# Moving the weight buffers and the activation buffers by 32 bytes in SBUF, in a two-block transformer kernel on one core

## The chip, the cores and the metric

The kernel runs on one core of a Trainium2 chip. The time is the device time of one launch in microseconds (us), lower is better. Three runs of the kernel before gave 3391.88, 3397.97 and 3398.14 us, median 3397.97 us.

## What is computed

Two blocks of depth 2 follow each other on an activation `x` of 256 tokens by 1024 channels, all in 32-bit floating point. Cut to what matters, with `modulated` a scaled and shifted RMS norm:

```python
# block 1, i = 0 and 1
x = x + 0.5 * gate * (silu(h @ w_gate) * (h @ w_up)) @ w_down      # h = modulated x, 1024 -> 2816 -> 1024
x = x + gate * (ssd_mixer(h) if i == 0 else mla_mixer(h))           # w_in, w_out
x = x + 0.5 * gate * (silu(h @ w_gate) * (h @ w_up)) @ w_down
# block 2, l = 0 and 1
x = x + gate * concat(rwkv7(h @ w_in), pool(h @ w_in)) @ w_out
x = x + gate * peer_ffn(h)     # queries, top 16 of 128 x 128 experts for each of 8 heads
# peer_ffn: act = gelu(h . peer_u[e]);  out = sum_e gate_e * act_e * peer_v[e]
```

The expert layer is computed densely here: all 16,384 rows of `peer_u` and of `peer_v` pass through TensorE, and the gates of experts that weren't chosen are zero.

## The kernel before

**Layout.** Activations stand with channels on the 128 partitions and the 256 tokens along the free axis, so one channel tile is 128x256, 1,024 bytes in each partition. Weights come from HBM as blocks of 128x1024 (512 KB, 4,096 bytes in each partition), one after the other over SyncE's queue, into slots: four slots of `ring`, and in some stages up to eight more (`MORE`) that lie inside `arena`, a buffer of 128 KB per partition that also holds every stage's temporary tensors. A block is eight 128x128 weight tiles of 512 bytes per partition.

**Weights in two parts.** Most products are made in the format fp32r, with one pass of TensorE instead of fp32's several, and in three parts so that the precision holds. ScalarE copies a block rounded to `weights_hi` (four buffers, line 1143). VectorE subtracts it from the block and leaves the rest, the low part, in place of the block (line 1638; `ring`, or `more_lo` for the slots in the arena). An activation is split the same way: `hh` (h_hi) and `h` (h_lo) for the normalized input of a stage, `small` (gat_hi) and `work` (gat_lo) for the gated activations that go into the second half of an FFN or of the expert layer.

**The matmuls around the change.** `columns_in_parts` (line 514) is the product of a weight block with the stage's input. For each of eight channel tiles it makes three matmuls of 128x256 moving columns: (high weights, `hh`), (high weights, `h`), (low weights, `hh`). `front` (lines 526, 527, 540) does the same for the first three blocks of a stage in another order. `rows_in_parts` (line 547) is the second half of an FFN and of the expert layer: three matmuls for each tile, with `small`, `work`, `small` as moving operands. In the output projections of two mixers (lines 681, 692 and 811) the moving operand lies in `more_lo`. Each of these matmuls loads its own 128x128 stationary tile (LDWEIGHTS, shown as PEld), and the load for the next one runs beside the current one.

**Order.** TensorE, ScalarE and VectorE each run a list in program order, bound by semaphores: a block's landing, its high part, its low part, its use (`block_used`, after which its slot may be filled again). In the four FFN stages VectorE also multiplies 56 blocks of modulation weights, which come over GpSimd's queue (line 1566). In the expert layers VectorE also does the routing (lines 2008 to 2075) and builds the gate matrix beside the first half (lines 2098 to 2113).

**Addresses.** `build` takes the buffers one after the other with `sb(...)`. Each begins at the next address that is a multiple of 32 bytes, so a buffer `[P, 2]` of 8 bytes moves what follows by 32 bytes. `sb_twice` lays a second view over the same bytes. In this kernel `ring` begins at byte 16,512 of a partition, which is a multiple of 128. The tiles that the matmuls named above read lie at multiples of 128 bytes from their buffer's start, so for them a whole buffer has one position modulo 128.

Of the kernel before, what the change touches and what calls it, by code (L numbers as in the profile page):

```python
# [8 lines left out]
F32R = mybir.dt.float32r  # L9
# [7 lines left out]
P = 128  # L17
D = 1024
T = 256
DT = D // P  # L20
# [246 lines left out]
def build(nc, stream, mods, cols_d, consts_d, x_d, pos_d, wuq_d, wukv_d, cond_d, keys_d, pool_d, lora_d, gup_d, vup_d, acts_d, out_d):  # L267
    with ExitStack() as ctx:
        def sb(name, shape, dt=F32):
            return ctx.enter_context(nc.sbuf_tensor(name, shape, dt))  # L270
# [6 lines left out]
        def sb_twice(name, shape, parts):  # L277

            with nc.sbuf_tensor(name, shape, F32) as whole:
                pass  # L280
            return whole, [sb(f"{name}_{i}", p, dt) for i, (p, dt) in enumerate(parts)]

        ring, (ring_lo,) = sb_twice("ring", [P, RING, 1024], [([P, RING, 1024], F32R)])
        whi = sb("weights_hi", [P, WS, 1024], F32R)
        with nc.sbuf_tensor("arena", [P, 128, 256], F32) as AR:
# [1 line left out]
        sb("arena_low", [P, 30, 256])  # L287
        more_lo = sb("more_lo", [P, MORE, 1024], F32R)
        sb("arena_high", [P, 128 - 30 - 4 * MORE, 256])
        x = sb("x", [P, DT, T])  # L290
        vfirst = sb("vfirst", [P, 4, T])
        cols = sb("cols", [P, NCOLS])
        kept = sb("kept", [P, KEPT])
# [2 lines left out]
        eps = sb("eps", [P, 20])  # L296
        modc = sb("modc", [P, NSUB, 24])
        omk = sb("one_minus_k_a", [P, 8])
        sb("ahead_of_activations", [P, 2])
        h, (h_lo,) = sb_twice("h", [P, DT, T], [([P, DT, T], F32R)])  # L300
        hh, (h_hi,) = sb_twice("hh", [P, DT, T], [([P, DT, T], F32R)])
        work, (_, gat_lo) = sb_twice("work", [P, 2048], [([P, 1024], F32), ([P, 4, T], F32R)])

        small, (gat_hi, _) = sb_twice("small", [P, 5, T], [([P, 4, T], F32R), ([P, T], F32)])

        ijg, rs, rv = small[:, 0:3, :], small[:, 3, :], small[:, 4, :]
        PS = ctx.enter_context(nc.psum_tensor("psum", [P, 8, 512], F32))
        acc = PS[:, 4:8, :].rearrange("p b (s t) -> p (b s) t", s=2)
# [2102 lines left out]
```

## Time and profile before

| | |
|---|---|
| median of three runs | 3397.97 us (3391.88 to 3398.14) |
| the profiled execution | 3391.88 us, span 3390.0 us |
| TensorE matmul busy | 3251.1 us, 96% |
| TensorE weight load busy | 3108.9 us, 92% |
| VectorE busy | 2581.1 us, 76% |
| ScalarE busy | 1608.2 us, 47% |
| mean granted TensorE clock | 0.987 of full speed |
| HBM traffic | 208 GB/s over the span |

The span runs from the first to the last instruction; 1.88 us of the profiled execution lie around it. The profiled execution is the fastest of the three runs, 6.1 us under their median. Rows of matmuls overlap in the profile: a row of 276 ns is followed by the next start 113 ns later, so what a stream of matmuls costs is read from the distance of starts, or from how many start in a stretch, not from the length of a row.

### The profile page before, as it was taken

The numbers are of one execution on the slowest core, as the hardware profiler recorded it, in microseconds if no ns is written. First come the engines' busy times: TensorE is split into PE (matmuls) and PEld (weight loads), VectorE is DVE, ScalarE is ACT, GpSimd is POOL, SyncE is SP. The second block draws the span as 40 slices with busy tenths as digits, with TensorE's granted clock in tenths as the row PEclk, the third lists the DMA queues.
The fourth block names the chain that finished last, engine by engine and source line by source line (L and its number), as shares of the span: only waits on it lengthen the run. The fifth ranks groups of instructions, "written<-read, shape, count | busy, mean of one in ns | idle before, by whom it ended". The sixth has DMA issues, their size and how long they took to land.

```text
span 3390.0 us, 68787 instructions
## 1 busy us (share of the span) xinstructions
PE 3251.1 (96%) x26804; PEld 3108.9 (92%) x26804; DVE 2581.1 (76%) x4576; ACT 1608.2 (47%) x2594; POOL 196.5 (6%) x331
## 2 busy tenths in 40 slices
PE   6999989999999998999999999998899999999998
PEld 5999769999867997989999999998789999999998
DVE  7989667989836997747978777776846978877777
ACT  3466644454445445144455444445325445544444
POOL 1100001111100111200000000000300000000000
PEclk8999999999999999999999999999999999999999
DMA  9964218979603973045755477774114665567775
GB/s 373 385 225 166 73 50 337 391 283 387 269 20 124 397 299 130 7 162 189 235 199 177 169 240 237 231 233 159 63 67 167 234 221 183 172 211 234 232 234 184
DMA packets 246578, 707.46 MB, mean 209 GB/s; under 512 B 27472, under 2 KB 93008, under 8 KB 244928
## 3 DMA queue, kind: packets, MB, share of 16 engines
q1 hardware_dynamic: 212112, 571.64, 48.4%
q0 software_dynamic: 34224, 132.46, 10.1%
q8 instruction: 167, 2.74, 0.3%
q14 instruction: 75, 0.61, 0.1%
HBM read 669.40 MB, written 34.60 MB: 208 GB/s over the span
## 4 chain that ended last, share of the span: by engine, by line
PE 81%; DMA 7%; DVE 6%; ACT 3%; issue 2%; SPq 0%; POOL 0%; DVEq 0%; ACTq 0%
PE psum L514 34%; PE psum L547 27%; DMA ring<-stream 6%; PE psum L1071 3%; PE psum L893 2%; PE psum L1006 1%; PE psum L644 1%; DVE ring L1638 1%; PE psum L913 1%; PE psum L495 1%; ACT weights_hi L1143 1%; PE psum L526 1%; PE psum L527 1%; DVE arena L1696 1%; PE psum L728 1%
## 5 line engine op out<-in xcount | busy, mean ns | idle before, releaser
L514 PE MATMUL psum<-hh,weights_hi 128*128 128x256 f32 x4216 | 1189.2, 282 | 24.5 <-DVE ring L1638 12.0
L1143 ACT ACTIVATE weights_hi<-ring 128x1024 fp32r<-128x1024 f32 x711 | 752.7, 1059 | 955.7 <-DMA ring<-stream 895.6
L1638 DVE TENSOR_TENSOR ring<-ring,weights_hi 128x1024 fp32r<-128x1024 f32 x711 | 870.2, 1226 | 409.5 <-ACT weights_hi L1143 404.6
L514 PE MATMUL psum<-h,weights_hi 128*128 128x256 f32 x4216 | 1172.2, 278 | 0.0
L514 PE MATMUL psum<-hh,ring 128*128 128x256 f32 x2976 | 829.0, 279 | 0.0
L514 PEld LDWEIGHTS psum<-hh,weights_hi 128*128 128x128 f32 x4216 | 796.6, 189 | 34.3 <-DVE ring L1638 17.2
L514 PEld LDWEIGHTS psum<-h,weights_hi 128*128 128x128 f32 x4216 | 798.7, 189 | 0.3
L547 PE MATMUL psum<-small,weights_hi 128*128 128x256 f32 x2752 | 768.8, 279 | 2.6 <-DVE ring L1638 1.6
L547 PE MATMUL psum<-work,weights_hi 128*128 128x256 f32 x2752 | 765.9, 278 | 0.0
L547 PE MATMUL psum<-small,ring 128*128 128x256 f32 x2304 | 642.2, 279 | 0.0
L514 PEld LDWEIGHTS psum<-hh,ring 128*128 128x128 f32 x2976 | 563.3, 189 | 0.0
L547 PEld LDWEIGHTS psum<-small,weights_hi 128*128 128x128 f32 x2752 | 520.5, 189 | 5.9 <-DVE work L2113 2.9
L547 PEld LDWEIGHTS psum<-work,weights_hi 128*128 128x128 f32 x2752 | 517.9, 188 | 0.0
L547 PEld LDWEIGHTS psum<-small,ring 128*128 128x128 f32 x2304 | 432.5, 188 | 0.0
L514 PE MATMUL psum<-hh,more_lo 128*128 128x256 f32 x1240 | 342.9, 277 | 0.0
L1638 DVE TENSOR_TENSOR more_lo<-arena,weights_hi 128x1024 fp32r<-128x1024 f32 x214 | 261.1, 1222 | 49.6 <-ACT weights_hi L1143 46.4
L1566 DVE SCALAR_TENSOR_TENSOR arena<-arena 128x1024 f32<-128x1024 f32 x232 | 282.3, 1219 | 5.1 <-DMA arena<-mod_weights 3.9
L1143 ACT ACTIVATE weights_hi<-arena 128x1024 fp32r<-128x1024 f32 x214 | 225.3, 1055 | 100.4 <-PE psum L514 75.3
L514 PEld LDWEIGHTS psum<-hh,more_lo 128*128 128x128 f32 x1240 | 232.8, 188 | 0.0
L2098 DVE TENSOR_SCALAR work<-kept,small 128x128 f32<-128x128 f32 x512 | 142.6, 343 | 71.2 <-PE psum L1071 65.9
L2109 DVE TENSOR_TENSOR work<-work,arena 128x256 f32<-128x256 f32 x256 | 159.6, 625 | 0.0
L2180 POOL DMA_DIRECT2D arena<-mod_weights x208 | 109.8, 528 | 529.9 <-DVE arena L1566 526.4
(410 smaller groups left out, 3894.0 us busy)
## 6 DMA issues: line engine op xcount, KB each, us to landing
ring<-stream SPq DMA_DIRECT2D x735, 512.0 KB, 3.9
arena<-mod_weights POOLq DMA_DIRECT2D x224, 512.0 KB, 7.0
arena<-stream SPq DMA_DIRECT2D x222, 512.0 KB, 6.4
acts<-small SPq DMA_DIRECT2D x256, 128.0 KB, 2.2
work<-acts SPq DMA_DIRECT2D x256, 128.0 KB, 3.0
arena<-cond_rows POOLq DMA_DIRECT2D x3, 1024.0 KB, 7.1
arena<-w_uq POOLq DMA_DIRECT2D x1, 3072.0 KB, 10.6
arena<-constants POOLq DMA_DIRECT2D x2, 1200.0 KB, 5.7
```

The source lines that it names most:

```text
L495: mm = pe.matmul(PS[:, 2, 0:T], ones, SQ[:, d, :], start=(d == 0), stop=(d == DT - 1))
L514: mm = pe.matmul(out, lhs[:, d, :], rhs[:, d, :], start=(d == 0 and p == 0), stop=(d == DT - 1 and p == 2))
L526: pe.matmul(out, w[:, d, :], h_hi[:, d, :], start=opens and d == 0, stop=False, skip_group_check=True)
L547: mm = pe.matmul(acc[:, d, :], lhs[:, d, :], rhs, start=False, stop=False, skip_group_check=True)
L893: mm = pe.matmul(PS[:, (4 * st + b) % 8, j * P:(j + 1) * P], lhs[:, c, :], rhs[:, c, :], start=True, stop=True)
L1071: mm = pe.matmul(PS[:, 4 + g % 4, j * P:(j + 1) * P], OHI[:, g % 2, j, :], OHJ[:, g % 2, j, :], start=True, stop=True)
L1143: act.activation(whi[:, NTH[n] % WS, :], raw(n), ACT.Copy).then_inc(sem["block_hi"], 1)
L1566: return dve.scalar_tensor_tensor(PRODUCT[:, m % 2, :], block, 1.0, COND[:, 0 if g < 6 else 1, :], ALU.mult, ALU.mult, accum_out=modc[:, g ...
L1638: dve.tensor_tensor(low(n), raw(n), whi[:, NTH[n] % WS, :].bitcast(F32), ALU.subtract)\
L2098: dve.tensor_scalar(OHI[:, g % 2, j, :], iota, ijg[:, 0, t:t + 1], ijg[:, 2, t:t + 1], ALU.is_equal, ALU.mult)
L2109: dve.tensor_tensor(gat[:, k % 4, :], sil[:, k % 4, :], WALL[:, :, i * 4 + k], ALU.mult).then_inc(sem["pe_gated"], 1)
L2180: pool.dma_start(MODRING[slot], mods[i * MOD_RING + (first + slot + MOD_RING)]).then_inc(mod_full[slot], 16)
```

## The change

Nothing is computed differently, no instruction is added or taken out, and no order, semaphore or DMA changes. Only the addresses of buffers in SBUF change.

```diff
+        sb("line_half", [P, 2])
         ring, (ring_lo,) = sb_twice("ring", [P, RING, 1024], [([P, RING, 1024], F32R)])
         whi = sb("weights_hi", [P, WS, 1024], F32R)
@@
         sb("arena_high", [P, 128 - 30 - 4 * MORE, 256])
+        sb("line_rest", [P, 2])
         x = sb("x", [P, DT, T])
+
+        h, (h_lo,) = sb_twice("h", [P, DT, T], [([P, DT, T], F32R)])
+        hh, (h_hi,) = sb_twice("hh", [P, DT, T], [([P, DT, T], F32R)])
         vfirst = sb("vfirst", [P, 4, T])
@@
         omk = sb("one_minus_k_a", [P, 8])
-        sb("ahead_of_activations", [P, 2])
-        h, (h_lo,) = sb_twice("h", [P, DT, T], [([P, DT, T], F32R)])
-        hh, (h_hi,) = sb_twice("hh", [P, DT, T], [([P, DT, T], F32R)])
+
         work, (_, gat_lo) = sb_twice("work", [P, 2048], [([P, 1024], F32), ([P, 4, T], F32R)])
```

The start of each buffer modulo 128 bytes, counted from the sizes above and the steps of 32:

| buffer | before | after |
|---|---|---|
| `ring`, `weights_hi`, `arena`, `more_lo` | 0 | 32 |
| `x` | 0 | 64 |
| `h`, `hh` | 64 | 64 |
| `vfirst`, `cols` | 0 | 64 |
| `kept` (identity, ones) and `zeros` | 96 | 32 |
| `work`, `small`, `ident_bf16` | 64 | 96 |

The moving operand's position less the stationary operand's, modulo 128, called the distance from here on:

| matmuls | before | after |
|---|---|---|
| lines 514, 526, 527, 540 (moving `hh` or `h`) | 64 | 32 |
| line 547 (moving `small` or `work`) | 64 | 64 |
| lines 681, 692, 811 (moving `more_lo`) | 0 | 0 |

## Rows read from the trace of the kernel before

**Rows 1.** The page: busy time of each engine (us, share, instructions).
```profile
PE 3251.1 (96%) x26804; PEld 3108.9 (92%) x26804; DVE 2581.1 (76%) x4576; ACT 1608.2 (47%) x2594; POOL 196.5 (6%) x331
```

**Rows 2.** The chain that ended last, in order of time: start us, us, what, whole span.
```profile
52.47 111.52 PE psum L514 x984
163.99 57.13 PE psum L547 x504
...
735.75 111.52 PE psum L514 x984
...
1567.34 4.25 DMA ring<-stream
...
1673.89 3.80 DMA ring<-stream
...
1687.00 37.03 PE psum L514 x312
...
2552.74 36.76 PE psum L514 x312
...
2597.37 121.56 PE psum L514 x1032
...
3019.82 266.38 PE psum L547 x2280
```

**Rows 3.** Groups by line, whole span: xcount | busy us, mean ns of one | idle before.
```profile
L514 PE MATMUL psum<-hh,weights_hi 128*128 128x256 f32 x4216 | 1189.2, 282 | 24.5 <-DVE ring L1638 12.0 <-ACT arena L1357 8.8 <-DVE more_lo L1638 1.9
...
L514 PE MATMUL psum<-h,weights_hi 128*128 128x256 f32 x4216 | 1172.2, 278 | 0.0
...
L514 PE MATMUL psum<-hh,ring 128*128 128x256 f32 x2976 | 829.0, 279 | 0.0
...
L514 PE MATMUL psum<-hh,more_lo 128*128 128x256 f32 x1240 | 342.9, 277 | 0.0
```

**Rows 4.** Timeline of TensorE at 120 us: start us, us, what.
```profile
119.74 0.28 PE L514 MATMUL psum<-h,weights_hi 128*128 128x256 f32 x1
...
120.99 0.28 PE L514 MATMUL psum<-hh,weights_hi 128*128 128x256 f32 x1
```

**Rows 5.** Timeline of TensorE at 510 us, distance 0.
```profile
509.79 0.28 PE L692 MATMUL psum<-more_lo,weights_hi 128*128 128x256 f32 x1
...
510.99 0.28 PE L692 MATMUL psum<-more_lo,ring 128*128 128x256 f32 x1
```

**Rows 6.** Groups by line from 60 to 160 us, matmuls.
```profile
L514 PE MATMUL psum<-hh,weights_hi 128*128 128x256 f32 x295 | 81.4, 276 | 0.0
```

**Rows 7.** Groups by line from 2570 to 2720 us, matmuls.
```profile
L514 PE MATMUL psum<-hh,weights_hi 128*128 128x256 f32 x403 | 113.3, 281 | 0.0
```

**Rows 8.** Groups by line from 490 to 528 us, matmuls.
```profile
L692 PE MATMUL psum<-more_lo,weights_hi 128*128 128x256 f32 x192 | 35.3, 286 | 4.7 <-DVE ring L1638 4.7
```

**Rows 9.** Stretches: us, busy and count of PE, PEld, DVE, ACT, POOL, then clock, DMA share, GB/s.
```profile
60.00:160.00 100.00, 100.00 (x885) 100.00 (x884) 94.52 (x137) 44.57 (x58) 19.34 (x37) 1.00 1.00 386
...
2600.00:2700.00 100.00, 100.00 (x851) 100.00 (x850) 89.34 (x377) 45.79 (x70) 0.00 (x0) 1.00 0.69 231
1960.00:2060.00 100.00, 100.00 (x851) 99.98 (x850) 74.17 (x106) 47.85 (x71) 0.00 (x0) 1.00 0.71 235
```

**Rows 10.** Timeline of TensorE at 1022 us, four transposes merged in one row.
```profile
1022.50 0.60 PE L783 MATMUL psum<-kept,arena 128*128 128x128 f32 x4
```

**Rows 11.** Groups by line from 1021 to 1027 us, the same transposes.
```profile
L783 PE MATMUL psum<-kept,arena 128*128 128x128 f32 x8 | 1.2, 272 | 0.0
```

**Rows 12.** Groups by line, whole span: two VectorE operations of one shape.
```profile
L2067 DVE TENSOR_TENSOR arena<-arena,kept 128x2048 f32<-128x2048 f32 x8 | 18.3, 2284 | 0.0
L2071 DVE TENSOR_TENSOR arena<-arena 128x2048 f32<-128x2048 f32 x8 | 18.3, 2284 | 0.0
```

**Rows 13.** The stretch of the second FFN's first half, line 514: us, PE, clock, DMA share, GB/s.
```profile
547.00:658.30 111.30, 110.71 (x976) 1.00 1.02 400
```

## The prediction

> **What bounds the kernel now.** I read the page first. TensorE is busy for 96% of the span and its weight loads for 92%, VectorE for 76% [rows 1]. Busy time can't tell a fast stream of matmuls from a slow one, since the rows overlap. So I went to the chain that ended last, in order of time, and divided each long piece by its count [rows 2]. The reader is to see long stretches in which nothing but TensorE's own pace sets the time: 984 matmuls in 111.52 us (113.3 ns each), twice, and 504 in 57.13 us (113.4 ns). But the same instruction is slower elsewhere: 312 in 36.76 us and 1032 in 121.56 us (117.8 ns both), 312 in 37.03 us (118.7 ns), and of line 547 2280 in 266.38 us (116.8 ns). The counts of whole stretches say the same: 885 matmuls in 100 us (113.0 ns) against 851 in 100 us (117.5 ns), all three at granted clock 1.00, the full 2.4 GHz, with TensorE busy throughout [rows 9]. So there are two paces of one instruction, about 113.3 and 117.8 ns, and neither clock nor waiting makes the difference.
>
> A third pace shows where the moving operand lies in `more_lo`: ten intervals in 510.99 - 509.79 = 1.20 us, 120 ns [rows 5], against eleven in 120.99 - 119.74 = 1.25 us, 113.6 ns by the rounded starts [rows 4]. The length of a row goes with the pace: 276 ns in the fast stretch, 281 in the slow one, 286 at line 692 [rows 6 to 8]. The last has distance 0, the first two distance 64. I read it as two streams out of SBUF, the moving tile and the next stationary tile, that get in each other's way, more or less according to where they lie. That the distance does it is my reading; line 692 differs from line 514 in its tensor too.
>
> The least pace that a 256-column matmul could have is bounded by rows in which nothing of this shows. Four fp32 transposes of 128 columns take 0.60 us [rows 10], each row 272 ns long [rows 11], so (600 - 272) / 3 = 109 ns apart. Scaling by columns is no help here, as fp32 takes more passes; but their row of 272 ns is 4 ns under the fast 276 and their pace 4 ns under 113.3, so I take 113.3 - 4 = 109.3 ns as the floor.
>
> The Trainium skill has a sentence on exactly this (TensorE: Matmul & The Clock Gate, Part 2, the step on LDWEIGHTS): "Loading the next tile's weights doesn't steal SBUF read bandwidth from the running matmul." Its gap for a warm 256-column matmul, N / 2.4 + 2.5, is 109.2 ns. The trace doesn't agree with the second: no stretch of line 514 runs under 113.0 ns [rows 9]. By the first, no placement of the two operands could matter, and the change would be worth nothing; that is the second rival below.
>
> **The change part by part.**
> (1) Lines 514, 526, 527, 540. Line 514 has 4216 + 4216 + 2976 + 1240 = 12,648 matmuls [rows 3]; `front` adds 24 x 3 x 10 = 720. Together 13,368. Their distance goes from 64 to 32. What pace have they now? The slow pieces in the chain hold 312 + 312 + 1032 = 1,656 [rows 2], smaller ones are cut off; I take 2,000, so the mean is 113.3 + 4.5 x 2,000 / 13,368 = 114.0 ns. Distance 32 stands nowhere in the trace for this instruction. Bounds: the floor 109.3 (gain 13,368 x 4.7 = 63 us) and the pace at distance 0, 120 (loss 13,368 x 6.0 = 80 us). The transposes are the nearest rows with half-way positions (`kept` at 96 against `arena` at 0), and show no collision; but their loads may differ, so they aren't proof. Between the ends far apart I choose by a supposition, not by a row: if the streams are read in pieces of 64 bytes, distances 0 and 64 both put the starts of the pieces on each other, and 32 is the first that puts them in between. I take the middle of the fast pace and the floor, 111.3 ns: 13,368 x 2.7 = 36 us gained.
>
> (2) Line 547, 3 x 8 x (4 x 22 + 2 x 128) = 8,256 matmuls. The distance stays 64; both operands move by 32. I price it at nothing. It can come out in either pace whatever the placement: 504 at 113.4 and 2280 at 116.8 exist side by side [rows 2]. If all ran fast, the second kind, some 3,700, would give back 17 us; if all ran slow, 4,500 more would cost 20 us.
>
> (3) Lines 681, 692, 811: distance 0 before and after, 576 matmuls, nothing.
>
> (4) VectorE, ScalarE, GpSimd. Every operand in the arena, `ring` and `weights_hi` moves from 0 to 32. An operation that reads `kept` (position 96) beside the arena takes 2284 ns, one of the same shape with the arena alone 2284 ns too [rows 12]. So nothing; and VectorE, with 74 to 94.5% busy [rows 9], would hide the first percent. Where it doesn't hide is the FFNs: at 94.5% their length can shrink by 5.5% at most, and the 1.8% of (1) fits, the 3.5% of the floor just does.
>
> (5) DMA. Weight blocks now land at 32 instead of 0. In the first half of an FFN the DMA engines are full (share 1.02, 400 GB/s) while TensorE is still busy for 110.71 of 111.30 us [rows 13]. No row shows a block landing at another position. Below, nothing; above, if each percent of slower landing came out in full in four such stretches, 4 x 111 x 1% = 4.5 us for a percent. I take nothing.
>
> (6) What isn't passed on. In the first expert layer's first half the chain goes through `DMA ring<-stream` again and again, in 13 pieces of about 4 us from 1567.34 to 1673.89 us [rows 2]. There a faster TensorE waits longer for its block. I take a tenth off: 36 becomes 32 us.
>
> Sum: the profiled execution 3391.9 - 32 = 3360 us. It lies 6 us under the median of its three runs, so against medians 3366; I put the forecast between, 3364 us, 1.0% faster than 3397.97.
>
> **The rivals.**
> *A, the collision falls at distance 32 (the forecast).* For it: the pace depends on placement at all, 113.3 against 120 [rows 4, 5], and nothing says that 64 is the best place. Against: only whole multiples of 64 have been seen. 3325 to 3385 us.
>
> *B, the placement isn't what sets the pace.* Then the three paces come from how the streams lock onto each other after a stall, and 120 at line 692 has another cause. For it: two paces at one and the same distance, [rows 6, 7]. The rule of the Trainium skill above leads here as well. Then the time moves only as the stretches fall into one pace or the other: all fast, -(2,000 x 4.5 + 17,000) ns = -26 us; all slow, 11,368 x 4.5 ns + 20 us = +71 us. The latter would need the FFNs too, which have kept the fast pace through 984 in a row twice. 3372 to 3420 us, the middle at 3398.
>
> *C, distance 32 collides like distance 0, on the other side.* The place is line 514, the price up to 6.0 ns for each of 13,368. At 120 ns 3398 + 80 = 3478 us; at 116.7, half-way between the paces at 64 and 0, 2.7 x 13,368 = 36 us, 3434 us. It decides from the point at which the mean pace of line 514 is over 114.5 ns (0.5 x 13,368 = 7 us, 0.2%). For it: if pace grows steadily from 113.3 at 64 to 120 at 0, then 32 lies between. Against: the two distances differ by half a period, and of two streams of unequal speed each crosses the other anyway, so a steady growth isn't given.
>
> **How the numbers follow.** A 0.41, B 0.29, C 0.30. A's time is the prediction. The range should leave out two in ten: below 3325 lies only the floor with line 547 all fast (0.03), above 3440 the worse half of C (0.14). So 3325 to 3440 us; A's own range is 3325 to 3385 us. 0.2% is about what a measurement can tell from no change here. Faster: A whole and 0.11 of B, 0.52; within 0.2%: 0.10 of B, 0.10; slower: C and 0.08 of B, 0.38.
>
> **What would show it.** From 60 to 160 us, with the same instructions, the count is now 885. At 111.3 ns it is 898, at 109.3 it is 915, at 120 it is 833. The mean row length of line 514 there goes from 276 towards 272 if A is right, towards 286 if C is. Under B it stays at 276 or jumps to 281. Line 692's starts stay 120 ns apart by (3), and line 547 keeps its paces of 113 and 118; if it has a third pace, the position and not the distance matters, and step (2) is wrong. Step (4) is wrong if line 1638 or 1143 changes its mean length. Step (5) shows in idle time of TensorE before line 514, released by the DMA, between 547 and 658 us. The prediction fails most easily in (1), whose price stands on no row of its own.

## The result, and the profile after

The changed kernel takes 3415.5 us (3415.0 to 3422.48 in three runs) against 3397.97 us before: ratio 1.0066, 95% interval 1.0049 to 1.0083. It is slower by 0.66%, where 1.0% faster was forecast. The profiled execution took 3425.5 us, with a span of 3423.6 us; it is a fourth one, 10 us above the median of the three, while the profiled execution before was 6 us under its median. In `kernel.py` the lines of these matmuls stand two further down than before: line 514 is now 516, line 547 is 549.

The chain of the changed kernel, in order of time (start us, us, what):

```profile
52.40 114.80 PE psum L516 x984
167.20 57.15 PE psum L549 x504
...
507.92 20.61 PE psum L694 x168
...
745.10 114.80 PE psum L516 x984
...
2042.97 238.87 PE psum L549 x2040
...
2580.35 36.41 PE psum L516 x312
...
2624.63 78.42 PE psum L516 x672
```

The two stretches of 984 matmuls, 113.3 ns each before [rows 2], now take 114.80 us, 116.7 ns each. The stretch of 504 in the FFN's second half, where the distance was kept, is unchanged at 113.4 ns. The 312 that were slow already (117.8 ns) are at 116.7 ns too. So in these stretches both old paces of the input products are gone and a new one is in their place. The stretches of time say the same (us, busy and count of PE, PEld, DVE, ACT, POOL, clock, DMA share, GB/s):

```profile
60.00:160.00 100.00, 100.00 (x859) 100.00 (x859) 91.79 (x132) 43.20 (x54) 18.75 (x36) 1.00 0.99 377
...
547.00:658.30 111.30, 110.99 (x950) 110.74 (x950) 100.84 (x146) 51.10 (x64) 19.41 (x37) 1.00 1.01 393
```

885 matmuls in 100 us have become 859 with TensorE busy throughout and the clock granted in full [rows 9], and 976 have become 950 in the second stretch [rows 13]. VectorE and the DMA do less per microsecond because they are asked for less. The groups by line, whole span, say what else moved:

```profile
L516 PE MATMUL psum<-hh,weights_hi 128*128 128x256 f32 x4216 | 1199.4, 284 | 25.0 <-DVE ring L1640 13.6 <-ACT arena L1359 9.0 <-DVE more_lo L1640 0.9
...
L1640 DVE TENSOR_TENSOR ring<-ring,weights_hi 128x1024 fp32r<-128x1024 f32 x711 | 871.7, 1228 | 422.4 <-ACT weights_hi L1145 418.5
...
L1145 ACT ACTIVATE weights_hi<-ring 128x1024 fp32r<-128x1024 f32 x711 | 753.7, 1061 | 970.4 <-DMA ring<-stream 913.3 <-PE psum L516 39.4 <-PE psum L549 17.3
```

The mean row of these matmuls is 2 ns longer than in [rows 3], the idle time in front of them is the same (25.0 against 24.5 us). VectorE's subtraction is 1228 ns against 1226 before, ScalarE's copy 1061 against 1059.

A steady stream is measured best by the distance of successive starts. I took all distances between two neighbouring matmuls of one line from the trace, for lines 514 and 540 ("input") and for line 547. Lines 526 and 527 take turns, so they have no such neighbours and are left out. A distance of up to 125 ns counts as steady, a longer one holds a wait. "All" is the sum over both kinds.

| | input, steady | mean ns | all, us | line 547, steady | mean ns | all, us |
|---|---|---|---|---|---|---|
| before | 12,432 | 114.26 | 1506.3 | 8,198 | 115.38 | 958.9 |
| after | 12,426 | 117.07 | 1542.0 | 8,177 | 114.70 | 957.1 |

12,426 x 2.81 ns = 34.9 us more for the input products, and 8,177 x 0.68 ns = 5.6 us less for line 547, together 29.3 us. "All" grew by 35.7 us, line 547 gave back 1.8 us, together 33.9 us; the span grew by 33.6 us. So between these two executions the loss lies in the pace of the input products. The medians differ by 17.5 us only; how much of a pace reaches the time is taken up further down.

### The profile page after: what moved, and what is told of

It is laid out like the page before. It is cut to its first block, busy times and chain, and to the rows that moved or that the text cites. A ratio compares the mean times of both kernels' runs of the same rounds, so it can differ in the third digit from the quotient of the medians.

```text
span 3423.6 us, 68787 instructions
## 1 busy us (share of the span) xinstructions
PE 3283.2 (96%) x26804; PEld 3139.6 (92%) x26804; DVE 2585.0 (76%) x4576; ACT 1610.8 (47%) x2594; POOL 197.3 (6%) x331
## 3 DMA queue, kind: packets, MB, share of 16 engines
q0 software_dynamic: 34224, 132.46, 10.2%
## 4 chain that ended last, share of the span: by engine, by line
PE 80%; DMA 8%; DVE 6%; ACT 3%; issue 2%; SPq 0%; DVEq 0%; POOL 0%; ACTq 0%; POOLq 0%
PE psum L516 35%; PE psum L549 25%; DMA ring<-stream 6%; PE psum L1073 3%; PE psum L895 2%; PE psum L1008 1%; PE psum L646 1%; DVE ring L1640 1%; ACT weights_hi L1145 1%; PE psum L915 1%; PE psum L497 1%; PE psum L528 1%; PE psum L529 1%; DVE arena L1698 1%; PE psum L730 1%
## 5 line engine op out<-in xcount | busy, mean ns | idle before, releaser
L1145 ACT ACTIVATE weights_hi<-ring 128x1024 fp32r<-128x1024 f32 x711 | 753.7, 1061 | 970.4 <-DMA ring<-stream 913.3
L1640 DVE TENSOR_TENSOR ring<-ring,weights_hi 128x1024 fp32r<-128x1024 f32 x711 | 871.7, 1228 | 422.4 <-ACT weights_hi L1145 418.5
```

The source lines that it names most:

```text
L1145: act.activation(whi[:, NTH[n] % WS, :], raw(n), ACT.Copy).then_inc(sem["block_hi"], 1)
L1640: dve.tensor_tensor(low(n), raw(n), whi[:, NTH[n] % WS, :].bitcast(F32), ALU.subtract)\
```

## The experiments

Two questions had to be told apart. Is it the distance that sets the pace, or the position, or the order of the buffers? And what is the rule by which distance becomes pace?

**A map of the paces.** The network is left out; the kernel only streams matmuls of the kernel's shape and format (256 columns, fp32r, each with its own stationary tile) from buffers at chosen bytes, and its output is just the input `x`.

```diff
-            # the network
+            def run_12(bank):  # stationary at byte 0, moving at byte 48
+                for r in range(3):
+                    for w, m in tiles(0, 12, 256):     # (high, act_hi), (high, act_lo), (low, act_hi)
+                        mm = pe.matmul(PS[:, bank, 0:256], w, m, start=True, stop=True)
```

> The disputed cost by itself. This kernel leaves the whole network out (its output is the input x); it streams fp32r matmuls of 128x256 in the order of line 514 (high weights with hi, high weights with lo, low weights with hi, eight tiles, three times over), 72 after a drained start and then three times 72 with one shorter matmul of 64, 144 or 200 columns ahead of each, for 32 distances in steps of 4 bytes with the stationary tiles at byte 0 of 128, and for a few with the stationary tiles at 16, 32, 64. If the distance modulo 128 sets the pace: 113.3 or 117.8 ns at 64, about 116.7 at 32, 120 at 0, and the same numbers again when the stationary tiles begin at 32 or 64 and the moving ones are moved along. If the position of the stationary tiles inside a 64-byte piece sets it (the rival): 116.7 at every distance with the stationary tiles at 32, at 113.3 or 117.8 for every distance with them at 0. If neither does: one pair of paces, 113.3 and 117.8, everywhere. No theory says what distances 96, 80 or 48 give; if the pace is even around 64 then 96 is like 32, 116.7.

There are four stretches of 72 matmuls for each placement. The first distances of a stretch are uneven, so here and in the other maps I give the mean of a stretch without its first twelve: 120 ns at distance 0; 116.7 to 117.8 at 32; 117.8 at 64; 120 at 96; 113.3 to 113.6 at 112; 113.3 or 118.6 at 16. Distances that are no multiple of 16 gave 116.9 to 123.4 ns. With the stationary tile at byte 32 these distances gave the same paces, in another mixture at 16. With it at byte 64, distance 64 gave 113.3 ns in the first of four stretches and 117.8 in the others. So 32 is a bad distance for every position tried. But 64 was bad too, 117.8 ns in all but that one stretch, where the kernel before ran at 113.3 and I had called its distance 64. One more point solved that: at 192 the map gives 113.3 ns in three of four stretches and 117.8 in the fourth. 64 and 192 are one distance modulo 128 and two modulo 256.

**Position alone.** All buffers move by 32 bytes, weights and activations, so that no distance changes.

```diff
+        sb("all_by_32", [P, 2])
         ring, (ring_lo,) = sb_twice("ring", [P, RING, 1024], [([P, RING, 1024], F32R)])
```

> The kernel before with one 32-byte step ahead of ring, and nothing else: every buffer moves by 32, the weights begin half-way in a 64-byte piece (byte 32 of 128), the activations at 96, both distances stay 64. If the distance sets the pace, line 514 keeps 113.3 ns in the FFNs (984 in 111.5 us) and the time is that of before, 3398 within 8 us. If the stationary tiles' own position costs, line 514 and line 547 both go to 116.7 and the time is 3398 + 13,368 x 2.8 + 8,256 x 1.3 ns, about 3446 us.

3400.81 us against 3403.24 us of the kernel before on the same chip, ratio 0.9999 (0.9983 to 1.0015); mean paces 114.53 and 115.41 ns. The time doesn't move by more than the interval. But the expected 984 matmuls in 111.5 us did not come in the first FFN:

```profile
52.60 115.89 PE psum L515 x984
```

That is 117.8 ns, while the 984 of the third FFN took 111.52 us. One placement can run at either of the two paces, and nothing here shows what decides it inside the kernel.

**The changed kernel with `h` and `hh` at distance 64 again.** If the period were 128, this would undo the harm and keep the order of the buffers.

```diff
+        sb("ahead_of_h", [P, 2])
         h, (h_lo,) = sb_twice("h", [P, DT, T], [([P, DT, T], F32R)])
@@
+        sb("ahead_of_work", [P, 24])
         work, (_, gat_lo) = sb_twice("work", [P, 2048], [([P, 1024], F32), ([P, 4, T], F32R)])
```

> The changed kernel with h and hh moved on by 32 bytes, so that their distance to the weights is 64 again, and with 96 bytes ahead of work so that line 547 keeps its distance of 64. The order of the buffers stays that of the change. If the distance of line 514 is the whole cause: back to 3398 within 8 us, 984 matmuls in 111.5 us. If the new order of the buffers (h and hh ahead of vfirst, other high address bits) has a share, the time stays between 3400 and 3417.

3433.67 us, ratio 1.0085 (1.0062 to 1.0108): nothing was undone. Its chain:

```profile
52.82 115.89 PE psum L518 x984
168.72 59.37 PE psum L551 x504
```

117.8 ns in both lines, in line 547 as well, which the change had left alone and which keeps its distance modulo 128 here. My reading of distances modulo 128 fell here.

**The kernel before with only `h` and `hh` moved by 32 bytes,** its order of buffers kept.

```diff
-        sb("ahead_of_activations", [P, 2])
         h, (h_lo,) = sb_twice("h", [P, DT, T], [([P, DT, T], F32R)])
         hh, (h_hi,) = sb_twice("hh", [P, DT, T], [([P, DT, T], F32R)])
+        sb("ahead_of_gated", [P, 2])
```

> The kernel before with the 32-byte step that stood ahead of h put behind hh instead: h and hh begin at byte 32, weights at 0, distance 32, and work and small stay exactly where they were. One part of the change alone. If the distance is the cause: slower like the change, 3413 to 3425 us, 984 matmuls of line 514 in 114.8 us. If the stationary tiles' half-way position is the cause: 3398, 111.5 us.

3431.64 us, ratio 1.0082 (1.0065 to 1.0099), 117.86 ns for the input products, 115.64 ns for line 547, which kept its place. One edit of 32 bytes for two buffers costs at least as much as the whole change. It isn't the same pace, though: the two stretches of 984 took 115.46 and 116.77 us where 114.8 was expected, and the time lies above the expected 3413 to 3425 us. Modulo 256 the distance is 160, not 32.

**The period.** The same map over 512 bytes, network left out as before.

> The same measurement (the network is left out, the output is x) over distances 0 to 496 bytes in steps of 16, with all four buffers at the same byte modulo 512, 48 matmuls in each of eight stretches that begin after matmuls of different lengths; then again with both operands moved by 32. In the first map distance 64 ran at 117.8 ns in 8 stretches of 8 and distance 192 at 113.3 in 3 of 4, and distance 0 at 120.0 against 118.7 at 128. If the period is 256 bytes: 64 and 320 alike (117.8), 192 and 448 alike (113.3), 32 and 288 alike (116.7), 160 like 416, about 117.9 from the kernel with h at 32. If the period is 128, as the prediction had it, and the two paces are a matter of the start alone, 64 and 192 show the same mixture of 113.3 and 117.8. If 512: 64 differs from 320.

It repeats every 256 bytes, stretch by stretch. The means of the eight stretches (48 matmuls each, without the first twelve distances) at some distances, in ns:

| distance | eight stretches |
|---|---|
| 0, 256 and 512 | 120.0 |
| 32 and 288 | 116.7 or 116.8 in four, 117.7 or 117.8 in four |
| 64 and 320 | 117.8 |
| 112 and 368 | 113.3 in six, 113.7 in two |
| 160 and 416 | 117.3 in five, 118.7, 118.7, 120.0 |
| 192 and 448 | 113.3 in five, 117.8 in three |

At distance 192 it is always the same three stretches that run at 117.8 ns, in this map and in the two other maps of this kind, on three chips: those that follow a matmul of 144, 32 or 176 columns. After one of 64, 200, 100 or 220 columns, and after a drained start, the pace is 113.3 ns. So the choice between the two paces isn't chance there; it repeats with what went before. The lengths came in the same order in every map, so the length itself isn't shown as the cause.

Counted modulo 256 from the buffers' addresses, the kernel before has distance 192 in both lines, the changed one 32 in the input products and still 192 in line 547, and the two kernels above 64, 64 and 160, 192. The table puts the distance of the kernel before ahead of the three others, as the times do.

**Two tests of the period in the kernel,** each with 128 bytes more ahead of the activations: the changed kernel's order with distance 192, and the kernel before with distance 64.

```diff
@@ changed kernel, h and hh back on distance 64, and 128 bytes more
-        sb("ahead_of_h", [P, 2])
+        sb("ahead_of_h", [P, 34])
@@ kernel before
-        sb("ahead_of_activations", [P, 2])
+        sb("ahead_of_activations", [P, 34])
```

> The kernel of run after_h_at_96 with 128 bytes more ahead of h, so that h, hh, work and small all move by 128 and nothing changes modulo 128. If the period is 128: 3433 within 8 us, line 514 at 117.8 ns in the FFNs. If it is 256: the distance is now 192 (that of the kernel before) for both, 984 matmuls of the FFN's first half in 111.5 us, 504 of its second half in 57.1, and the time is back at 3402 within 8 us, with the order of buffers of the change.

> The kernel before with the buffer ahead of h made 128 bytes larger and nothing else: h, hh, work and small move by 128 together. If the period is 128: the time of before. If it is 256: both distances go from 192 to 64, every stretch locks into 117.8 ns, 984 in 115.9 us and 504 in 59.4, about 3434 us.

The first: 3394.71 us, ratio 0.9985 (0.9968 to 1.0002), paces 113.99 and 114.45 ns. The second: 3427.89 us, ratio 1.0087 (1.0057 to 1.0117), paces 117.10 and 117.43 ns. Chain of the first, then of the second, with the first and the third FFN:

```profile
52.28 111.52 PE psum L518 x984
163.79 57.13 PE psum L551 x504
```

```profile
52.77 115.89 PE psum L514 x984
168.66 59.37 PE psum L547 x504
...
751.34 111.52 PE psum L514 x984
```

128 bytes make the harmed kernel whole and harm the good one. The new order of buffers shows no cost. Not every stretch came to 117.8 ns in the second, as was expected: the 984 of the third FFN ran at 113.3. So 64 and 192 have the same two paces, and differ in how often each comes.

**The worst place.** Distance 0 modulo 256 for both lines, by a pad of 96 bytes.

```diff
-        sb("ahead_of_activations", [P, 2])
+        sb("ahead_of_activations", [P, 24])
```

> The kernel before, with the activations moved so that moving minus stationary is 0 modulo 256 bytes for the input products and line 547 alike. If the map of paces holds inside the kernel: nearly all of the 12,400 steady input products go from 114.3 to about 120 ns and the 8,200 of line 547 from 115.4 to about 120 ns: 3398 + 12.4 x 5.7 + 8.2 x 4.6 = 3398 + 71 + 38 = 3507 us, ratio about 1.03; VectorE and the DMA queues have more slack, so none of it is hidden. If the placement matters only through which pace a stretch falls into (113.3 or 117.8), at most 3398 + 12.4 x 3.5 + 8.2 x 2.4 = 3461 us and no stretch at 120 ns.

3477.98 us, ratio 1.0248 (1.0222 to 1.0274); 119.90 and 119.98 ns. All of the expected pace came, and 82 of the expected 109 us by the medians of this set. The chain, and the same hundred microseconds as above:

```profile
52.72 118.08 PE psum L514 x984
170.80 60.49 PE psum L547 x504
```

```profile
60.00:160.00 100.00, 100.00 (x836) 100.00 (x835) 89.58 (x128) 41.37 (x53) 18.49 (x35) 1.00 0.99 365
```

The steady starts cost 12,492 x 5.64 + 8,239 x 4.60 = 108.4 us more, "all" only 85.8 us, and the span 86.0 us. The 23 us between are waits between these matmuls that a slower TensorE no longer has.

**Better places.** Distance 112 with the stationary tile at 0 modulo 32, and distance 192 with it at 16 modulo 32. Buffers begin at multiples of 32, so the 16 bytes are taken inside one larger buffer:

```diff
-        sb("ahead_of_activations", [P, 2])
-        h, (h_lo,) = sb_twice("h", [P, DT, T], [([P, DT, T], F32R)])
+        sb("ahead_of_activations", [P, 48])
+        acts, (acts_r,) = sb_twice("activations", [P, 8 + 3 * 2048 + 1280], [...])
+        h, h_lo = (acts[:, 4:4 + 2048] ..., acts_r[:, 4:4 + 2048] ...)       # 4 elements = 16 bytes in
```

This is the edit for distance 112, cut and simplified; `hh`, `work` and `small` follow in the same buffer. For the other placement the weights too lie 16 bytes inside larger buffers.

> The kernel before with h, hh, work and small in one buffer that begins 16 bytes past a multiple of 32, so that the distance of lines 514 and 547 is 112 in place of 192; the weights stay where they were. The maps had 113.3 to 114.3 ns at 112 in all stretches and no lock at 117.8. If the pace of the stream in the maps carries over to the kernel: mean pace 113.8 on both lines against 114.3 and 115.4 before, 12,400 x 0.5 + 8,200 x 1.6 ns = 19 us, about 3383, and runs that scatter less than the 3389 to 3417 of the kernel before. If waits and the other engines' traffic break the order of the streams up, a mean near 115 and no gain over before.

> The same measurement (the network is left out, the output is x) with the stationary tiles at byte 16, where the other maps had them at 0 and 32, over distances 0 to 240; then distance 112 with the stationary tiles at 0, 32, 48, 64 and 96, and distances 192, 64 and 0 again; last, distances 0, 64, 32 and 192 with stationary tiles of 64 columns in place of 128, so that the load beside each matmul is half as long. If two streams out of SBUF collide, the matmul that runs beside a load of half the length loses less: its pace goes from 120, 117.8, 116.7 and 113.3 towards the 109 ns of the transposes at all four distances. If the moving stream alone sets the pace, 64 columns change nothing. Distance 112 keeps 113.3 to 114.3 ns in all eight stretches wherever the stationary tiles begin, if the distance alone counts.

> The kernel before, with the weights (ring, weights_hi, more_lo, arena) at byte 144 modulo 256 and the activations at 80, so the distance stays 192 as before but the stationary tiles start at byte 16 modulo 32, where the map showed 113.3 to 114 ns in all eight stretches (with the stationary tiles at 0 modulo 32 it was 113.3 in five of eight and 117.8 in three). If the map holds in the kernel, the input products come to about 113.5 ns (from 114.3) and line 547 to about 113.5 (from 115.4): 3398 - 12.4 x 0.8 - 8.2 x 1.9 = 3398 - 10 - 16 = 3372 us if all of it is passed on, 3376 to 3384 with a part lost to the other engines, as with distance 112. If only the distance counts and not where the stationary tile starts: same as before, 3398 us within 0.2%.

Distance 112: 3383.5 us, ratio 0.9966 (0.9949 to 0.9982), faster than the kernel before; 113.90 and 113.60 ns. The map with the stationary tile at byte 16 (network left out): distance 192 gives 113.3 ns in all eight stretches, distance 112 now gives 118.3 to 120.0. With the stationary tile at 0, 32, 64 or 96 distance 112 keeps 113.3 to 113.7 ns, at 48 it gives 116.7 to 120.0. So the stationary tile's byte modulo 32 counts beside the distance. What was expected of stationary tiles of 64 columns failed: they should have brought all four distances towards 109 ns, and gave 113.3 at distance 0, 116.7 at 64, 116.7 to 119.1 at 32 and 119 at 192. The kernel built on the first part took 3386.18 us, ratio 0.9965 (0.9949 to 0.9981), with 113.68 and 113.47 ns: the pace that was expected, but 10 us of the 14 to 26 expected.

Where the rest went shows in the page's shares of the chain, here of distance 112:

```profile
PE 77%; DMA 10%; DVE 6%; ACT 4%; issue 3%; SPq 1%; DVEq 0%; POOL 0%; ACTq 0%; POOLq 0%
PE psum L519 33%; PE psum L552 23%; DMA ring<-stream 8%; PE psum L1076 3%; PE psum L898 2%; PE psum L1011 1%; ACT weights_hi L1148 1%; PE psum L649 1%; DVE ring L1643 1%; PE psum L918 1%; PE psum L500 1%; PE psum L531 1%; PE psum L532 1%; DVE arena L1701 1%; PE psum L733 1%
```

The stream of weight blocks holds 8% of the chain; in the kernel before it was 5.6%, and TensorE 81% instead of 77%. In the second half of the first expert layer, from 1950 to 2330 us, the stream's share of the chain goes from 2.5% to 16.0%.

**How much of a pace reaches the time.** With the stationary tiles at 16 the steady starts save 12,402 x 0.58 + 8,169 x 1.91 = 22.8 us, but "all" (1509.6 and 947.8 us) is only 7.8 us under before; the medians of that set differ by 10.2 us. The same for the other kernels, the paces from one profiled execution of each and the medians from all, in us:

| kernel | steady starts | median |
|---|---|---|
| the change | +29.3 | +17.5 |
| `before_plus_128` | +52.3 | +25.8 |
| `before_h_at_32` | +47.1 | +28.4 |
| `after_h_at_96` | +55.0 | +30.4 |
| `distance_0` | +108.4 | +81.6 |
| `all_by_32` | +3.6 | -2.4 |
| `after_h_at_minus_64` | -11.0 | -7.4 |
| `distance_112` | -18.9 | -13.9 |
| `stationary_at_16` | -22.8 | -10.2 |

Leaving out `all_by_32`, which is within the noise, 45% to 75% of a change of pace arrives, in both directions. These are rough shares, since single executions of one kernel scatter by some 10 us about the median. By the traces the rest lies in waits between the matmuls: with the stationary tiles at 16, 22.8 less 7.8 us.

**What collides.** The network is left out once more; four distances with four kinds of operands.

```diff
+    plain:       lhsT = w[:, a:a + 128],                 rhs = m[:, b:b + 256]
+    narrow:      lhsT = w[:, a:a + 32]
+    one_column:  lhsT = w[:, a:a + 1].to_broadcast([P, P])
+    one_token:   rhs  = m[:, b:b + 1].to_broadcast([P, n])
```

> Network left out; only streams of 192 matmuls (8 weight tiles of 1024 columns in three products, as in the kernel) at distances 0, 64, 32 and 192 bytes, in four kinds: plain; a stationary tile of 32 columns; a stationary tile that is one column read 128 times; a moving operand that is one column read 256 times. Plain: 120, 113.3 or 117.8, 116.7, 113.3 ns, as in the maps before. Theory 'two reads of the on-chip memory meet': with the moving operand a single column its reads stay in one place and the pace no longer depends on the distance, all four distances within 1 ns of each other; the same with the stationary tile a single column; with 32 columns of weights the pace falls towards 109 to 111 ns at all distances, as there are four times fewer loads' reads to meet. Rival 'the pace depends on the start addresses through something other than the data read' (how the instruction is set up): the spread over the distances stays, 113 to 120 ns, in all four kinds.

Stretches of 48 in the chain. A piece holds the slow first starts of its stretch too, so its time over 48 lies above the pace that the stretch settles at; compare the pieces with each other. First plain at distance 64 (line 107), then plain at 192 (line 153):

```profile
109.78 5.72 PE psum L107 x48
...
115.58 5.68 PE psum L107 x48
```

```profile
202.24 0.05 PE psum L165
202.29 5.53 PE psum L153 x48
...
207.89 5.69 PE psum L153 x48
```

and with one token as the moving operand, at distance 0 (line 360), 64 (line 383) and 32 (line 406):

```profile
604.94 5.45 PE psum L360 x48
610.39 0.05 PE psum L372
610.44 5.42 PE psum L360 x48
...
649.25 5.45 PE psum L383 x48
...
654.75 5.42 PE psum L383 x48
...
693.56 5.45 PE psum L406 x48
...
699.06 5.42 PE psum L406 x48
```

By distances of starts, with the moving operand one repeated column: 111.7 ns in all 32 stretches, the same at all four distances. The start addresses are the same as in the plain kind, so the rival, that the start addresses act through something other than the data read, is out. With the stationary tile one repeated column the distance still shows: 113.3 ns at 192 in every stretch, while single stretches at 0 and 32 go up to 120.0. With 32 columns: 113.3 or 117.8 at distance 0, 117.3 or 120.0 at 32. So the pace hangs on the addresses that the moving operand is read from, and the dependence on the distance is gone when it does not walk through memory. That was the theory's half. The other half came in part: fewer or unmoving reads of the stationary tile don't clear it, and 109 to 111 ns was not reached by them. But they change it. With one repeated column five of the eight stretches at distance 0 went from 120.0 to 113.3 ns, and six of the eight at 64 from 117.8 to 113.3; with 64 columns of weights all eight at distance 0 did, while those at 192 went up to 119. So what the weight load reads does take part in the pace; how, stays open.

## Why the prediction was wrong, step by step

**Step (1) failed, in its sign.** It priced the distance 32 at 111.3 ns by the supposition that streams are read in pieces of 64 bytes, of which 32 is the middle. Measured: 117.07 ns in the kernel, 116.7 in its long stretches and in four of eight in the map (116.7 or 116.8). 34.9 us of pace were lost where 36 were to be gained. The bounds, 109.3 and 120 ns, held, and the measured time lies inside the stated range; that is owed to the range's width, which took in most of C, and not to the mechanism. Two readings under it were false:
- *The period.* I counted distances modulo 128, because that put lines 514 and 692 on two tidy values. They are 192 and 0 of 256. Nothing in the trace of before showed 64 of 256, which runs at 117.8 ns nearly everywhere; I took the pace of 192 for that of 64. With two known points there was no ground for any period, nor for an interpolation.
- *The floor.* 109.3 ns came from fp32 transposes. No placement of two full operands got a whole stretch under 113.3 ns, in the maps or in the kernel. Only the repeated moving column did, 111.7. The fast pace of before was already the best that was found, and a change of placement could win back only the slow stretches. The Trainium skill's gap of N / 2.4 + 2.5, 109.2 ns here (TensorE: Matmul & The Clock Gate, Part 2, Back-to-back issue gap), isn't met by any fp32r stream here. The page gives it for an isolated matmul and says that in a stream with a weight load beside each matmul both set the spacing.

**The mean pace now** was put at 114.0 ns; 114.26 measured.

**Step (2)** held: line 547 went from 115.38 to 114.70 ns, 5.6 us less over its steady starts and 1.8 us less over all; it fell into its fast pace somewhat more often, at an unchanged distance. Moving everything by 32 bytes gave 115.41 ns, so no effect of the position shows at this line.

**Step (3)** held: the steady starts of lines 681, 692 and 811, now 683, 694 and 813, are 119.89 ns apart before and after.

**Step (4)** held: 1226 to 1228 ns for 711 subtractions is 1.4 us, beside TensorE's work.

**Step (5)** held: in the stretch from 547 us TensorE is busy for 110.99 of 111.30 us, and waits for no block.

**Step (6)** was mis-sized. A tenth was taken off for one stage; by the medians 25% to 55% of a change of pace is lost on the way, of a gain as of a loss, and here 12 of 29 us. By the two profiled executions nothing of this loss was hidden, but one of them was a quick one of its kernel and the other a slow one. The expert layers' stream of weights takes far more than a tenth as soon as TensorE gets faster: at distance 112 its share of the chain from 1950 to 2330 us went from 2.5% to 16.0%.

**The rivals.** C was right in the place and in the sign: distance 32 collides, it gave 3434 us at a mean pace of 116.7 ns and decided from 114.5 ns. That its 116.7 is the pace measured is luck. It was the half-way value between two distances, as A's 111.3 was, and the map doesn't go evenly between them: 113.3 ns for some stretches at 16, 118.3 at 48, and the pace taken for that of 64 is that of 192. The measured 3415.5 us lie 18 us under its time, mainly because it passed the whole pace on to the time, where 17.5 of 29.3 us arrived. I set C back with the remark that the two distances differ by half a period, which stood on the same false period. B is half true: two paces at one distance exist in the maps (113.3 and 117.8 ns at 192, by what a stretch follows) and in the kernels, where nothing but the position moved and the first FFN went from 113.3 to 117.8 ns; but the placement decides which paces are to be had and how often. The rule that leads to B, that loading the next tile doesn't take read bandwidth from the running matmul (the Trainium skill, the same page, Part 2, the step on LDWEIGHTS), does not cover what was measured: 113.3 to 120 ns for the same instructions by their addresses alone. A would need a stretch of two full operands under 113.3 ns, and none was found.

**The signs.** The count from 60 to 160 us is 859, between the 833 of C at 120 ns and the 885 of no change, and the row length there went from 276 to 279 ns, towards C's 286. Both signs pointed to C, and line 547 has no third pace.

## What to carry to other kernels

- The start of the moving operand less that of the stationary one is a parameter of a tuned stream of matmuls: here the worst place costs 2.5% and the best one found wins 0.35%. Measure it with a map of a few dozen lines before moving a buffer; don't interpolate between two points.
- Count addresses modulo more than the rule you suspect, and name the position that no row shows. A pad or a new order of buffers ahead of them shifts it unseen.
- Ask what a faster bound engine runs into: here 10 of 23 us arrived. And compare medians: a single profiled execution of each kernel can be off by more than the effect.

## What the runs showed of the hardware that was not expected

- The pace of 256-column fp32r matmuls with a 128x128 load each repeats with the distance every 256 bytes: 120 ns at 0, 117.8 and seldom 113.3 at 64, 113.3 or 117.8 at 192, 113.3 to 113.7 at 112.
- Which of its two paces a stream at distance 192 keeps repeats with what went before, the same on three chips: 117.8 ns after a matmul of 32, 144 or 176 columns, 113.3 after one of 64, 100, 200 or 220.
- The stationary tile's start modulo 32 counts too: with it at 16, distance 112 goes to 118.3 to 120.0 ns and 192 is at 113.3 in every stretch. Distances that are no multiple of 16 bytes ran at 116.9 to 123.4 ns.
- A smaller load is not always better: with 64 instead of 128 columns of weights, distance 0 went from 120 to 113.3 ns and distance 192 from 113.3 or 117.8 to 119.0.
- With one repeated column as the moving operand the pace is 111.7 ns at every distance tried.
